# An expert weight piece near the end of the stream, loaded as 96 rows and four times eight rows

## The reference, cut to what matters

```python
D_MODEL, SEQ, N_EXPERTS, TOP_K, D_FF_EXPERT = 1024, 256, 32, 4, 1024

x = x + (g_a * y_a + g_b * y_b) @ w_out[l]
x = x + moe_ffn(rms_norm(x, norm2_g[l]), w_router[l], b_router[l], w_gate_up[l],
                b_gate_up[l], w_down[l], b_down[l])
...
def expert_block(args):
    tok, e = args
    hgu = xt[tok] @ w_gate_up[e] + b_gate_up[e]          # 1024 -> 2048
    gate = jnp.minimum(hgu[:, 0::2], SWIGLU_LIMIT)
    up = jnp.clip(hgu[:, 1::2], -SWIGLU_LIMIT, SWIGLU_LIMIT)
    act = gate * jax.nn.sigmoid(SWIGLU_ALPHA * gate) * (up + 1.0)
    return act @ w_down[e] + b_down[e]                   # 1024 -> 1024
```

## Time and profile before

| | |
|---|---|
| median of 3 runs | 1246.1 us (1243.53 to 1246.5) |
| profiled execution, its own time | 1245.76 us |
| its span | 1243.9 us |
| TensorE matmuls (PE) | 1192.9 us busy, 96% of the span |
| gate_up matmuls, L1626 | 469.7 us, idle before them 25.2 us, of it 23.7 on ring<-w_gate_up |
| down matmuls, L1651 | 219.2 us, idle before them 6.3 us, all on ring<-w_down |
| SP queue's transfers (q1) | 440.36 MB, 84.4% of the 16 DMA engines' time |
| a 4096 KB piece, issue to landing | 36.0 us (w_gate_up, x55), 33.8 us (w_down, x28) |

### The profile page before, as it was taken

How to read it: one execution, slowest core, us unless ns; L and a number is a source line. 1 busy time by engine, 2 the same in 40 slices (tenths; PEclk the granted TensorE clock), 3 DMA queues, 4 the chain that set the end, 5 groups by cost and what they waited for, 6 DMA issues and landing times.

```text
span 1243.9 us, 16239 instructions
## 1 busy us (share of the span) xinstructions
PE 1192.9 (96%) x7258; PEld 571.0 (46%) x7258; DVE 293.2 (24%) x644; ACT 187.1 (15%) x358; POOL 7.8 (1%) x18
## 2 busy tenths in 40 slices
PE   7999999999999999999998989999999999898997
PEld 5788578875533333433333333334333333333332
DVE  2166454343321112211111111111211111111111
ACT  3353212234110100000100000000000000010002
POOL 0000000000000000000000000000000000000000
PEclk9999999999999999999999999999999999999999
DMA  8332655349999999999999999999999999999994
GB/s 298 131 124 86 219 179 159 112 175 407 353 412 411 429 431 433 428 435 428 432 429 432 430 432 432 428 436 426 432 432 429 436 425 435 428 431 433 429 424 176
DMA packets 34748, 448.83 MB, mean 361 GB/s; under 512 B 11328, under 2 KB 11600, under 8 KB 18416
## 3 DMA queue, kind: packets, MB, share of 16 engines
q1 hardware_dynamic: 24336, 440.36, 84.4%
q10 hardware_dynamic: 9040, 3.01, 1.0%
q0 software_dynamic: 1296, 4.34, 1.0%
HBM read 445.61 MB, written 2.10 MB: 360 GB/s over the span
## 4 chain that ended last, share of the span: by engine, by line
PE 72%; DMA 26%; DVE 1%; issue 0%; ACT 0%; DVEq 0%; ACTq 0%
PE ps L1626 27%; DMA ring<-w_gate_up 26%; PE ps L1235 8%; PE ps L1651 8%; PE ps L1326 7%; PE ps L1611 5%; PE ps L1680 3%; PE ps L1313 2%; PE ps L1511 2%; PE ps L1634 2%; PE ps L1670 1%; PE ps L1661 1%; PE ps L1265 1%; PE ps L1575 1%; DMA consts<-cst 1%; PE ps L1364 0%
## 5 line engine op out<-in xcount | busy, mean ns | idle before, releaser
L1626 PE MATMUL ps<-ring,xacc 128*64 128x512 f32 x2048 | 469.7, 606 | 25.2 <-DMA ring<-w_gate_up 23.7
L1626 PEld LDWEIGHTS ps<-ring,xacc 128*64 128x64 f32 x2048 | 143.8, 138 | 315.9 <-issue 309.6
L1651 PE MATMUL ps<-ring,aT 128*64 128x512 f32 x992 | 219.2, 594 | 6.3 <-DMA ring<-w_down 6.3
L1651 PEld LDWEIGHTS ps<-ring,aT 128*64 128x64 f32 x992 | 74.1, 137 | 147.3 <-issue 147.3
L1187 DVE TENSOR_SCALAR gc<-ps 128x512 f32<-128x512 f32 x32 | 22.1, 692 | 392.1 <-PE ps L1626 392.1
L1143 DVE TENSOR_TENSOR xacc<-ps,consts 128x512 f32<-128x512 f32 x32 | 22.1, 692 | 345.5 <-PE ps L1611 345.5
L1235 PE MATMUL ps<-hT,wbuf 128*128 128x256 f32 (+1 forms) x432 | 99.4, 388 | 0.8 <-DVE hT L837 0.8
L1235 PEld LDWEIGHTS ps<-hT,wbuf 128*128 128x128 f32 (+1 forms) x432 | 80.8, 190 | 18.1 <-issue 5.0
L1326 PE MATMUL ps<-hT,wbuf 128*128 128x256 f32 x384 | 85.6, 381 | 0.0
L1326 PEld LDWEIGHTS ps<-hT,wbuf 128*128 128x128 f32 x384 | 72.1, 190 | 11.4 <-issue 1.8
L796 ACT ACTIVATE sgm<-gc 128x512 f32<-128x512 f32 x32 | 20.2, 630 | 371.6 <-DVE gc L1187 371.6
(11 more groups left out here) (246 smaller groups left out, 664.5 us busy)
## 6 DMA issues: line engine op xcount, KB each, us to landing
ring<-w_gate_up SPq DMA_DIRECT2D x55, 4096.0 KB, 36.0
ring<-w_down SPq DMA_DIRECT2D x28, 4096.0 KB, 33.8
ring<-w_gate_up SPq DMA_DIRECT2D x16, 2048.0 KB, 11.1
wbuf<-w_in SPq DMA_DIRECT2D x25, 512.0 KB, 3.4
wbuf<-w_in SPq DMA_DIRECT2D x12, 1024.0 KB, 5.5
ring<-w_down SPq DMA_DIRECT2D x6, 2048.0 KB, 11.7
wbuf<-w_in SPq DMA_DIRECT2D x2, 2048.0 KB, 8.3
wbuf<-w_out SPq DMA_DIRECT2D x8, 512.0 KB, 5.3
```

The source lines that it names most:

```text
L1626: last = mm(bank(GU_BANK + q, 0, 512, slice(64 * half, 64 * half + 64)), x_, w[:, :, half, :], start=k == 0, stop=k == KT - 1, skip_group_ ...
L1651: last = mm(bank(b, 0, 512, slice(64 * half, 64 * half + 64)), turned[:, c0:c0 + SLOTS], w[:, D * r + 512 * half:D * r + 512 * (half + 1)] ...
```

## The change

Piece 90 (`UNEVEN = PIECES - 6`) is no longer one transfer of 128 rows. It is a transfer of rows 0 to 95, followed by four transfers of eight rows: 96 to 103, 104 to 111, 112 to 119, 120 to 127. All five come from SP's queue, one behind the other, after the same wait, read the same bytes and write the same place. `fills(90)` becomes 5, so that TensorE waits for all five. Nothing else is changed.

```diff
+        UNEVEN = PIECES - 6
...
         def fills(n):
-            return 4 if n == RING else 2 if n < 2 * RING else 1
+            return 4 if n == RING else 2 if n < 2 * RING else 5 if n == UNEVEN else 1
...
+            def load_rows(n):
+
+                for lo, hi in [(0, 96)] + [(r, r + 8) for r in range(96, P, 8)]:
+                    sp.dma_start(ring[slot_of(n)][lo:hi, :], pieces[n][lo:hi, :]).then_inc(ring_full[slot_of(n)], 16)
...
                         if n in TAIL_PARTS:
                             load_tail(n)
+                        elif n == UNEVEN:
+                            load_rows(n)
                         else:
                             load(n, 0, PIECE, ring_full[slot_of(n)])
```

## The result

The change makes the kernel slower: 1272.74 us (median of 6 runs, 1267.84 to 1275.23) against 1245.41 us before (6 runs, 1243.53 to 1246.5), a ratio of 1.0219 with a 95% interval of 1.0208 to 1.0229, or +27.3 us. The forecast had the sign and the kind of cost, and half of the size; its range ended at 1271.

The account below looks back on a forecast made before the run. The prediction took the landing of piece 92 plus 46.4 us of PE work as the bound. Profiled 1245.8 + 0 (issues) + 0 (semaphore) + 14 (eight-row transfers) = 1259.8, so 1260 us; range 1245 to 1271.

Parts of the forecast that it names:

- What bounds the kernel: Around piece 90 the weight stream decides: the end is the landing of piece 92 plus PE's remaining work.
- 46.4 us of work: PE's own work between the landing of piece 92 and the end of the span, taken as unchanged.
- Issues and semaphore at 0: Four more issues on SP and PE's wait for five landings in place of one were each to cost 0.
- On 16 engines six rows each, 7.3 us instead of 9.7: The transfer of 96 rows of piece 90 was to take 2.4 us off every engine.
- Four times eight rows, 19.5 to 24.4 us: Eight neighbouring rows reach two write lanes of 27 GB/s; four such transfers add +17 to +22 us on eight engines.
- If they are the half that is 5.5 us ahead, the landing moves by the rest: If the eight engines run 5.5 us ahead, piece 90's landing moves +11.5 to +16.5 us, middle +14.
- Rival A: The eight-row transfers go to the late half of the engines: +17 to +22 us, say 1265.5 us; chance 0.12.
- B: No lanes, each engine writes at its own rate, the eight are the half ahead: 1243.8 us; chance 0.12.
- C: No lanes: late half +2.4 us, 1248.2, chance 0.05; different engines each time, no change, 1245.8, chance 0.05.
- D: Four lanes for eight neighbouring rows: +7.4 us on the eight engines, 5.5 hidden, +2, 1248 us; chance 0.10.
- E: One lane for eight neighbouring rows: +36.6 us less 5.5, +31, 1277 us; chance 0.06.
- The stop of 12 us in the middle of expert 30: Expected sign: PE stops about 12 us before the second half of expert 30, waiting for piece 90.

Follow-up runs that it names:

- five_full: Kernel before, with piece 90 in five transfers split by columns, each over all 128 rows: 1245.46 us for 1245.85 before, ratio 0.9997.
- marks: Kernel before, with a tiny eight-row transfer behind pieces 20, 45, 70 and 90 in SP's queue to show when its engines pass: 1245.49 us for 1245.5.
- in quiet: Kernel before, plus whole pieces loaded after its last store with nothing else in flight: 33.74 us split as in the change, 12.50 as 128 rows.
- at piece 20: The change made to piece 20 in place of piece 90: 1268.97 us for 1245.5 before, ratio 1.0198.
- small_spread: Kernel before, with piece 90 as 128 rows by 6144 columns, the other columns in 16 transfers of eight rows four apart: 1253.08 us, ratio 1.0057.

## Why the prediction was wrong, point by point

- **What bounds the kernel** held: the stops before pieces 91 and 92 are unchanged, PE is bound by the landing of piece 92, and nearly all of the loss is waits for transfers before it. The "46.4 us of work" behind that landing are not fixed, though: here they are 44.7 (1266.0 less 1221.33). The x24 stretch of expert 31 took 7.07 us before, at a granted clock of 0.57 in the mean from 1198 to 1202, and takes 5.37 now, at 1.00. Piece 92 itself lands at 1221.20, 23.9 us later than before.
- **Issues and semaphore at 0** held (five_full; the five issues took 1.75 us, the 1.7 foretold).
- **"On 16 engines six rows each, 7.3 us instead of 9.7"** failed, and is the first wrong step. I applied the lanes to the eight-row transfers only and left the 96 rows at the engines' rate, in the same text that read from the earlier trace rows that half of the rows take no more than half of the rate. It measured 14.3 us. By itself: +7.0 us. Counting lanes would have mended only a part: with eight rows in the fullest of them it gives the 9.7 us of 128 rows, and no row of before shows the rest.
- **Four times eight rows, 19.5 to 24.4 us** was mis-sized the other way: 16.8 us together, middle of the estimate 21.9, so -5.1 us. Two lanes for eight neighbouring rows is right: eight rows took as long as four, and 2.5 us more than eight rows spread.
- **"If they are the half that is 5.5 us ahead, the landing moves by the rest"** failed, and is the second wrong step. It failed twice over. The eight engines are not the half ahead: two of them are late (marks), and the piece lands with the last engine, 4.7 us behind the other fourteen in the change. And I saw the lead as time to spare, while engines that are ahead and write the split piece slow those behind: the late half took until 46.2 us for piece 89 where it took 40.3. So in place of -5.5 us the stream added 6.1 (27.3 by the medians, 21.2 in quiet; about 1 in the profiled execution; 2.3 at piece 20).
- The sum with the measured terms: 19.5 (the forecast's own +17 to +22) + 7.0 - 5.1 = 21.4, the quiet +21.2; with +6.1 in place of -5.5 it is +27.5. That last step is no check, since the 6.1 are the measured time less the quiet one; the 21.4 are. **Two errors of one sign and one of the other.**
- **Rival A** (the eight rows go to the late half) was right for two of the eight engines, and these two are enough to lose the lead. Its +17 to +22 held the quiet +21.2 by chance: the 7.0 us missed on 96 rows and the 5.1 too many on the eight-row transfers offset each other. **B** and **C** (no lanes) are refuted by the quiet times. **D** and **E** too: two lanes.
- **The stop of 12 us in the middle of expert 30** came, with 14.93; the stop before expert 30 was listed as what "wrong altogether" would look like (PE stops at pieces before 90). It was the sign of the second error.
- **The range** gave 0.12 to going 5 us beyond the forecast and 0.06 to more. It took its width from the count of lanes and from which half the engines are, and none from the 96 rows or from what the halves do to each other.

Shown: the written rows set the rate; 96 rows cost 14.3 us; 9 us of the loss hang on neighbouring rows; engines behind are slowed as soon as others are at the split piece; for 96 and 32 rows the surplus is larger where the engines are further apart. Argued, not shown by itself: that this happens because engines of both groups are in one lane, and that the last two engines are the late ones with more rows. Open: how the surplus divides between the two, and why five of the six runs of the changed kernel are 4 to 7 us slower than the profiled one.

Could the idea be made to work? No split tried here gained anything, and the best of the uneven ones (small_spread) lost 7.2 us. Rows that other engines take over still have to be written into the same lanes; that this rules the idea out is argued, not shown.

## What to carry to other kernels

In a stream that is bound by its transfers, keep every transfer on all 128 partitions and split by columns if it must be split: that was free here, five parts and all, while every split that put some of it on fewer rows cost 7 to 27 us for a single 4 MB piece. When a limit is found on one side of a transfer, apply it to every transfer of the change, the big one first, and price a mixed form by the lane that gets most rows, not by the engines. Even that is a lower bound: it gives 9.7 us for 96 rows, and 14.3 were measured, so time a new form alone first. A lead of some engines is no slack unless all the extra work goes to them, and not even then once they slow those behind.

## What was not expected of the hardware

- 96 rows of 32 KB take longer than 128 of them: 16.72 against 12.11 us from issue to issue, alone in the queue; and 64 rows take as long as 128 (12.74).
- Four neighbouring rows take as long as sixteen (6.34 and 6.49 us), four rows spread four apart take 3.85.
- A transfer can be slowed by what stands behind it in the same queue: piece 89 landed after 46.22 us for 40.3, and the engines that were late are those that had not ended it when the others went on to piece 90.
